# Adding the experts' rows to the residual rows in memory by accumulating transfers, instead of gathering and adding them afterwards

## The chip, the cores and the metric

The kernel runs on one core of a Trainium2 chip. The metric is the device time of one execution in microseconds, the median of three runs. TensorE is called PE here, VectorE DVE, ScalarE ACT, GpSimd POOL and SyncE SP. SBUF is the on-chip memory with 128 partitions, PSUM the memory that TensorE writes to, and HBM the large memory outside. A DMA is a transfer by the core's 16 DMA engines. It is issued by the queue of SP, ACT or POOL.

## What is computed

One transformer block with a mixture of experts is followed by a second block, whose mixer is a short convolution. All arithmetic is float32, 1024 tokens of width 1024. The part that the change touches is the routed experts, the sum of their rows into the residual stream, two norms and the first product of the second block:

```python
def expert_block(args):            # one block of 128 rows, all of one expert
    xb, e = args
    g = xb @ w_gate[e]
    u = xb @ w_up[e]
    return (jax.nn.silu(g) * u) @ w_down[e]

ys = lax.map(expert_block, (xs, block_expert)).reshape(rows, d)
out = jnp.zeros((t, d), h.dtype).at[row_token].add(ys * row_weight[:, None])
...
x = x + gate2[:, None, :] * moe
return rms_norm(x, final_norm_g)
# second block
h = modulate(rms_norm_2(x, norm_gains[i, 0]), sh_m, sc_m)
bcv = h @ w_in                     # 1024 x 3072, then the convolution
```

Each token goes to 2 of 32 experts (`TOP_K` = 2), so 2048 rows are spread over blocks of 128 rows; a block belongs to one expert and what it has over is padding. With the inputs used here 32 blocks are computed.

## The kernel before

The kernel is written by hand, engine by engine; each engine's program is a fixed list with semaphore waits, and there is no scheduler. It consists of stages, each a `nc.Block()`, which ends with a barrier of all engines: diff_attention, mla_attention, attention_out, route, experts, combine_conv, conv_out_ffn. Behind mla_attention and route stands `clear_sems` (L58), which clears the used semaphores on POOL and has a further barrier of all engines.

Products in float32 precision are made of three passes (`three_passes`, L115): each operand is split into a leading part (an ACT copy to the type fp32r) and a rest (a DVE subtraction). So every weight piece that comes from memory costs one ACT instruction and one DVE instruction before TensorE can use it.

**mla_attention.** While the attention runs, SP fills 34 blocks of the memory tensor `y_rows` with zeros (L1009, four transfers of 4352 KB).

**route (L1702).** DVE works out the experts, weights and destinations of all tokens in a chain of small instructions. Last come the list of tokens of each block (`g.rows`) and the expert of each block (`g.blocks`, from a comparison of 48 x 32 elements on one partition, L1866). SP waits for `g.blocks` and loads the first four weight pieces (L1885); POOL waits for `g.rows` and gathers the first two blocks of token rows by indirect DMAs (L1893).

**experts (L1897).** A loop on each engine, two blocks per round. One block has 12 weight pieces of 512 KB (8 of gate and up, 4 of down). SP loads a piece into one of 12 slots of `e_raw` as soon as DVE has used the slot's last content (`low`). ACT and DVE split it into one of 6 slots of `e_w` (L2122, L2058), TensorE multiplies (72 products of 128x512 for a block, besides 12 transposes). DVE's `copy_y` (L2080) takes the block's result out of PSUM, multiplied by the gate row, into `e_yo`. ACT's `store_y` (L2142) waits for that copy and issues a plain transfer of the 128 rows to `y_rows`. POOL only gathers the token rows of a block two ahead (L1990, L1993).

**combine_conv (L2188).** POOL gathers for each of 8 tiles of 128 tokens the two rows of each token from `y_rows` (16 indirect DMAs, L2263). DVE multiplies each by its weight and adds it to the residual rows (`add`, L2434 and L2437). ACT and DVE make two norms (`square_sum`, `norm`, `square_normed`, `inverse`, and ACT's `scaled`, L2353). TensorE turns the rows (`turn_half`, L2284), ACT applies scale and shift (`affine`, L2363), DVE splits (`split`, L2457 and L2459), and the first column of the input product (`f` = 0) follows. All of this goes by halves of 512 tokens: the product of a half waits until all its 8 chunks of 128 channels are split. The scale and shift come from two sums over partitions on TensorE (L69), whose operands SP loads in this stage, behind the three weight pieces of `f` = 0.

## Time and profile before

| | us |
|---|---|
| median of 3 runs | 2646.66 (2643.35 to 2647.84) |
| the profiled execution | 2647.36 |
| its span (first to last instruction) | 2645.7 |
| PE busy | 2383.6 (90%) |
| DVE busy | 1732.2 (65%) |
| ACT busy | 1229.3 (46%) |
| POOL busy | 452.0 (17%) |
| mean granted TensorE clock | 0.945 of full speed |

Times in rows count from the first instruction of the span. A row of the timeline gives the start, the duration, the engine, the line of the code, the operation, `output<-inputs`, the number of instructions, and in brackets how long the engine had been idle before and what ended that. "SPq", "ACTq" and "POOLq" are rows of an engine's queue: issues of transfers, drains and semaphore events. A share of the DMA engines is the time that packets took, added up over 16 engines, by 16 times the stretch. With all queues added it can come out a little above 100%.

### The profile page before, as it was taken

How to read it: one execution, taken by the hardware profiler on the slowest of the kernel's cores; microseconds unless marked ns; L12 is line 12 of the kernel's file. 1: busy time of each engine (PE TensorE's matmuls, PEld its weight loads, DVE VectorE, ACT ScalarE, POOL GpSimd, SP SyncE). 2: the span in 40 equal slices, each digit the busy share in tenths (PEclk: the TensorE clock that was granted, in tenths of full speed). 3: DMA queues.
4: the chain of work that ended last, by engine and by line, in shares of the span. 5: the costliest groups of instructions: out<-in, count | busy, mean ns of one | idle time of the engine just before them, and what ended most of it. 6: DMA issues, size and time to landing. Idle time of an engine off the chain costs nothing. (4 is left out here: it accounts for less than half of the span.)

```text
span 2645.7 us, 31508 instructions
## 1 busy us (share of the span) xinstructions
PE 2383.6 (90%) x10764; PEld 1908.4 (72%) x10764; DVE 1732.2 (65%) x1998; ACT 1229.3 (46%) x1643; POOL 452.0 (17%) x396
## 2 busy tenths in 40 slices
PE   5989986898897599999999569997999999999998
PEld 4667764676576488777877358886777888888886
DVE  6378884656585699999999655444447666653344
ACT  5246664565422477777676451110564333332332
POOL 0000001887200110000000200000013333221100
PEclk8999986999897799999999779998999999999999
DMA  6131121339464699999999844332423223245453
GB/s 242 28 119 49 41 87 51 97 90 340 138 204 159 243 399 398 399 398 398 399 398 399 311 153 119 112 104 79 160 76 84 79 76 91 71 139 176 149 169 116
DMA packets 266072, 485.30 MB, mean 183 GB/s; under 512 B 19633, under 2 KB 125566, under 8 KB 265470
## 3 DMA queue, kind: packets, MB, share of 16 engines
q1 hardware_dynamic: 232734, 364.37, 39.6%
q0 software_dynamic: 26912, 98.62, 11.2%
q10 hardware_dynamic: 6336, 21.11, 2.0%
q8 instruction: 57, 0.93, 0.1%
q14 instruction: 33, 0.27, 0.0%
HBM read 402.24 MB, written 76.55 MB: 181 GB/s over the span
## 5 line engine op out<-in xcount | busy, mean ns | idle before, releaser
L2058 DVE TENSOR_TENSOR e_w<-e_raw,e_w 128x1024 fp32r<-128x1024 f32 x384 | 441.9, 1219 | 55.0 <-ACT e_w L2122 54.8
L2122 ACT ACTIVATE e_w<-e_raw 128x1024 fp32r<-128x1024 f32 x384 | 376.5, 1051 | 186.0 <-PE e_pgu L119 146.2
L119 PE MATMUL e_pgu<-e_w,e_xt 128*128 128x512 f32 x1536 | 368.1, 396 | 11.1 <-DVE e_w L2058 5.5
L119 PEld LDWEIGHTS e_pgu<-e_w,e_xt 128*128 128x128 f32 x1536 | 285.3, 189 | 85.8 <-DVE e_w L2058 18.3
L119 PE MATMUL s_ps<-h,s_w 128*128 128x512 f32 x1152 | 266.8, 394 | 5.0 <-DVE h L2459 5.0
L119 PEld LDWEIGHTS s_ps<-h,s_w 128*128 128x128 f32 x1152 | 218.8, 190 | 51.8 <-DVE h L2459 5.6
L119 PE MATMUL w_ps<-w_out,w_ring 128*128 128x512 f32 x1056 | 244.1, 390 | 2.1 <-DVE w_ring L3095 2.1
L119 PE MATMUL w_ps<-y 128*128 128x512 f32 x1056 | 240.1, 389 | 1.4 <-DVE w_o_full L3260 1.0
L119 PEld LDWEIGHTS w_ps<-w_out,w_ring 128*128 128x128 f32 x1056 | 198.1, 188 | 45.1 <-DVE w_out L3102 2.9
L119 PEld LDWEIGHTS w_ps<-y 128*128 128x128 f32 x1056 | 197.9, 188 | 43.5 <-issue 1.4
L119 PE MATMUL w_ps<-y,w_ring 128*128 128x512 f32 x816 | 196.0, 398 | 4.3 <-ACT w_h L2892 3.0
L119 PE MATMUL e_py<-e_w,e_att 128*128 128x512 f32 x768 | 186.1, 398 | 3.7 <-DVE e_att L2075 3.7
L119 PEld LDWEIGHTS w_ps<-y,w_ring 128*128 128x128 f32 x816 | 154.2, 189 | 42.2 <-ACT w_h L2892 3.2
L119 PEld LDWEIGHTS e_py<-e_w,e_att 128*128 128x128 f32 x768 | 143.9, 191 | 33.5 <-issue 4.0
L119 PE MATMUL ad_pj<-h,ad_w 128*128 128x512 f32 x576 | 144.6, 406 | 4.7 <-ACT ad_spare L502 4.7
L3248 DVE TENSOR_TENSOR y<-w_o_full,y 128x1024 fp32r<-128x1024 f32 x44 | 53.9, 1225 | 143.6 <-ACT y L3032 143.6
L119 PEld LDWEIGHTS ad_pj<-h,ad_w 128*128 128x128 f32 x576 | 108.2, 192 | 38.9 <-issue 7.5
L3032 ACT ACTIVATE y<-w_o_full 128x1024 fp32r<-128x1024 f32 x44 | 46.6, 1060 | 161.4 <-PE w_ps L119 161.4
L2899 ACT ACTIVATE w_ring<-w_h 128x512 fp32r<-128x512 f32 x80 | 50.3, 632 | 143.6 <-PE w_ps L119 132.7
L3095 DVE TENSOR_TENSOR w_ring<-w_raw,w_ring 128x512 fp32r<-128x512 f32 x76 | 88.1, 1187 | 24.5 <-ACT w_ring L2899 24.5
L119 PE MATMUL w_ps<-w_out,y 128*128 128x512 f32 x384 | 94.5, 406 | 9.6 <-DVE w_out L3077 9.4
L1990 POOL COPY e_idx<-rows 128x1 uint32 x30 | 16.4, 546 | 468.0 <-PE e_px L2001 468.0
(402 smaller groups left out, 3904.4 us busy)
## 6 DMA issues: line engine op xcount, KB each, us to landing
e_raw<-in_w_expert_gate_dram SPq DMA_DIRECT2D x128, 512.0 KB, 12.7
e_raw<-in_w_expert_up_dram SPq DMA_DIRECT2D x128, 512.0 KB, 12.4
e_raw<-in_w_expert_down_dram SPq DMA_DIRECT2D x128, 512.0 KB, 12.2
w_raw<-in_ffn_w_gate_up_dram SPq DMA_DIRECT2D x48, 512.0 KB, 5.9
w_o_full<-in_ffn_w_down_dram SPq DMA_DIRECT2D x44, 512.0 KB, 4.0
y_rows<-am_zrow SPq DMA_DIRECT2D x4, 4352.0 KB, 34.7
raw_rows<-in_w_ada_dram POOLq DMA_DIRECT2D x32, 512.0 KB, 3.9
y_rows<-e_yo ACTq DMA_DIRECT2D x32, 512.0 KB, 6.3
```

The costliest lines, as they stand in the source:

```text
L119: o = pe.matmul(out, stat[i], mov[j], start=start and n == 0, stop=stop and n == 2)
L1990: pool.tensor_copy(idx[b][:], g.rows[:, ds(2 * i + b, 1)]).then_inc(idx_ready, 1)
L2058: dve.tensor_tensor(w[1][:, slot % CUT], raw[:, slot], w[0][:, slot % CUT].bitcast(F32), ALU.subtract).then_inc(low, 1)
L2122: act.activation(w[0][:, slot % CUT], raw[:, slot], ACT.Copy).then_inc(high, 1)
L2899: act.activation(ring[0][:, to], src, ACT.Copy).then_inc(high, 1)
L3032: act.activation(d_w[0][t % 2].rearrange("p (c n) -> p c n", c=2), d_raw[t % 2], ACT.Copy).then_inc(d_high, 1)
L3095: dve.tensor_tensor(ring[1][:, to], src, ring[0][:, to].bitcast(F32), ALU.subtract).then_inc(low, 1)
L3248: dve.tensor_tensor(d_w[1][t % 2].rearrange("p (c n) -> p c n", c=2), d_raw[t % 2], d_w[0][t % 2].rearrange("p (c n) -> p c n", c=2).bitca ...
```

## The change

- `y_rows`, its zero fill, the 16 gathers and the 16 DVE additions of combine_conv are gone. The memory tensors `h2_rows` and `x_rows` get 128 more rows, which take what padding rows read and write; 8 transfers clear them in mla_attention.
- route makes a further table: the weight of each slot of each block (`weight_of`, 16 products on TensorE, `g.weight_at`). The expert of each block is worked out with the blocks over the partitions (`ended`, `owner`), turned by one product (`pow_`), and stands ready before the destinations of the tokens are worked out.
- In experts `copy_y` multiplies by the slot's weight as well. ACT's `store_y` is gone. POOL scatters each block's rows by an indirect DMA with `compute_op=ALU.add` onto the residual rows in memory (`scatter`). Each scatter waits for the copy of its block and for the landing of the scatter before, since a token can be in two blocks. SP loads the residual rows when both last scatters have landed; the operands of the two sums and the gain row are loaded before that.
- combine_conv begins with the two sums. The unit rows are made by DVE (`scaled`, `tensor_scalar`) instead of ACT. TensorE turns chunk by chunk into five places of PSUM, and the product of `f` = 0 goes chunk by chunk, three columns to each, as soon as a chunk is split.
- `clear_sems` is gone; POOL clears the semaphores in the stage that follows, without a barrier of its own.

```diff
@@ mla_attention, SP
-                    sp.dma_start(g.y_dram.rearrange("(n p) (c q) -> c p n q", p=P, c=4)[q, :, MIN_BLOCKS:],
-                                 zrow[:].unsqueeze(1).broadcast_to([P, Y_BLOCKS - MIN_BLOCKS, D // 4])).then_inc(g.zeroed, 16)
+                    for rows in (g.h_dram, g.x_dram):
+                        sp.dma_start(rows[T:T + P, q * (D // 4):(q + 1) * (D // 4)], zrow[:]).then_inc(g.zeroed, 16)
@@ route, DVE
+                seq(dve.tensor_scalar(ended[:], inc[:], tok[:, NT + 1:NT + 2], None, ALU.is_le))
+                seq(dve.tensor_reduce(owner[:], ended[:], AX_X, ALU.add))
+                dve.tensor_scalar(owner[:], owner[:], float(EXPERTS - 1), None, ALU.min).then_inc(owners, 1)
...
+                dve.tensor_copy(g.blocks[0:1, 0:MAX_BLOCKS], pow_[0:1, 0:MAX_BLOCKS]).then_inc(known, 1)
...
+                dve.tensor_tensor(weight_of[:], at_block[:], bc(g.wt[:].rearrange("p s n -> p (s n)"), MAX_BLOCKS), ALU.mult).then_inc(spread, 1)
@@ experts, POOL
+                def scatter(j, b, others):
+                    pool.wait_ge(y_copied, j + 2)
+                    if not (isinstance(j, int) and j == 0):
+                        pool.wait_ge(y_out[1 - b], 16 * others)
+                        pool.sem_inc(y_free, 1)
+                    pool.tensor_copy(idy[b][:], g.rows[:, ds(j, 1)]).then_inc(idy_ready, 1)
+                    pool.wait_ge(idy_ready, j + 1)
+                    pool.sem_inc(idx_seen, 1)
+                    pool.indirect_dma_start(g.x_dram, bass.IndirectOffsetOnAxis(ap=idy[b][:], axis=0), yo[:, b, :], None,
+                                            compute_op=ALU.add).then_inc(y_out[b], 16)
...
+                with pool.Fori(0, n) as i:
+                    gather(2 * i + 6, 0)
+                    scatter(2 * i + 2, 0, i + 1)
+                    gather(2 * i + 7, 1)
+                    scatter(2 * i + 3, 1, i + 2)
@@ experts, DVE and ACT
-                    dve.tensor_tensor(yo[:, b, :], py[:], g.gate[:, 1, :], ALU.mult).then_inc(y_copied, 1)
+                    dve.wait_ge(y_free, j + 1)
+                    dve.scalar_tensor_tensor(out=yo[:, b, :], in0=py[:], scalar=g.weight_at[:, ds(j, 1)], in1=g.gate[:, 1, :],
+                                             op0=ALU.mult, op1=ALU.mult).then_inc(y_copied, 1)
...
-                def store_y(j, b):
-                    act.wait_ge(y_copied, j + 2)
-                    act.dma_start(y_rows[ds(j, 1)].squeeze(0), yo[:, b, :]).then_inc(y_out[b], 16)
@@ combine_conv, TensorE
+                for c in range(KD):
+                    turn(c)
+                pe.wait_ge(col_out, 1)
+                pe.wait_ge(low, 6)
+                for k in range(KD - 1):
+                    first_products(0, k)
+                turn(KD)
+                turn(KD + 1)
+                first_products(0, KD - 1)
...
@@ combine_conv, ACT (the order until the first affine)
+                columns()
                 square_sum(0)
                 square_sum(1)
                 square_normed(0)
                 square_sum(2)
                 square_normed(1)
-                scaled(0)
                 square_sum(3)
                 square_normed(2)
-                scaled(1)
                 leading(0, 0)
                 square_normed(3)
-                scaled(2)
                 leading(0, 1)
-                scaled(3)
-                columns()
-                affine(0)
+                square_sum(4)
                 leading(0, 2)
-                square_sum(4)
+                for c in range(4):
+                    affine(c)
```

The first place is POOL's loop in experts. `e_xg` is the buffer of token rows, `e_yo` the block's result, `x_rows` the residual rows in memory. Before, one round is:

```order
L1990 ISA
L1990 COPY e_idx<-rows 128x1
L1993 DMA e_xg<-h_rows,e_idx 128x1024
L1988 REGISTER_ALU
L1990 ISA
L1990 COPY e_idx<-rows 128x1
L1993 DMA e_xg<-h_rows,e_idx 128x1024
```

And now:

```order
L2003 COPY e_idx<-rows 128x1
L2006 DMA e_xg<-h_rows,e_idx 128x1024
L2009 REGISTER_ALU
L2011 ISA
L2013 ISA
L2013 COPY e_idy<-rows 128x1
L2014 REGISTER_ALU
L2016 DMA x_rows<-e_yo,e_idy 1152x1024
L2001 REGISTER_ALU
L2003 ISA
L2003 COPY e_idx<-rows 128x1
L2006 DMA e_xg<-h_rows,e_idx 128x1024
```

Between two gathers POOL now has the wait for a block's copy, the wait for the scatter before, and a scatter.

The second place is ACT's loop in experts, at the end of a block. `e_att` is the turned activation, `e_w` the leading parts of the weights. Before:

```order
L2138 ACTIVATE e_att<-e_pa 128x512
L2142 ISA
L2142 DMA y_rows<-e_yo 128x1024
L2121 REGISTER_ALU
L2122 ACTIVATE e_w<-e_raw 128x1024
```

And now:

```order
L2180 ACTIVATE e_att<-e_pa 128x512
L2163 REGISTER_ALU
L2164 ACTIVATE e_w<-e_raw 128x1024
L2163 REGISTER_ALU
L2164 ACTIVATE e_w<-e_raw 128x1024
```

The issue of the store, with its wait for DVE's copy, is out of ACT's queue, so that the next weight piece follows the activation directly.

The third place is TensorE at the start of combine_conv. `s_ps` and `s_pm` are PSUM, `s_mrows` and `column_parts` the operands of the two sums, `h_room` unit rows, `h_0`, `h_1` and `s_w` the split operands. Before:

```order
L69 MATMUL s_ps<-ones,s_mrows 128x1 x16
L2284 MATMUL s_pm<-ident,h_room 128x128 x32
L119 MATMUL s_ps<-h_0,s_w 128x512 x2
L119 MATMUL s_ps<-h_1,s_w 128x512
L119 MATMUL s_ps<-h_0,s_w 128x512 x2
```

And now:

```order
L60 MATMUL s_ps<-ones,column_parts 128x1 x16
L2305 MATMUL s_pm<-ident,h_room 128x128 x8
L2305 MATMUL s_ps<-ident,h_room 128x128 x12
L2305 MATMUL s_pm<-ident,h_room 128x128 x8
L2305 MATMUL s_ps<-ident,h_room 128x128 x4
L110 MATMUL s_ps<-h_0,s_w 128x512 x2
L110 MATMUL s_ps<-h_1,s_w 128x512
```

The order on TensorE up to the first product is nearly the same; the turned chunks go to more places, and the products behind it now run over the chunks first.

## Rows read from the trace of the kernel before

**Rows 1.** DMA of the stretch 890 to 1480 (experts): queues, then issues with us to landing.

```profile
DMA packets 96386, 233.92 MB, mean 396 GB/s; under 512 B 7040, under 2 KB 7040, under 8 KB 96379
...
q1 hardware_dynamic: 87739, 202.38, 90.3%
q0 software_dynamic: 4320, 15.73, 6.8%
q10 hardware_dynamic: 4320, 15.73, 6.6%
...
y_rows<-e_yo ACTq DMA_DIRECT2D x30, 512.0 KB, 6.3
...
e_xg<-h_rows,e_idx POOLq DMA_INDIRECT x30, 7.8
```

**Rows 2.** Landing times of weight pieces (tile e_raw) issued in 932 to 1000.

```profile
DMA to landing us min/median/max: 10.6/12.9/14.5
```

**Rows 3.** The same for pieces issued in 1400 to 1500.

```profile
DMA to landing us min/median/max: 9.1/11.9/14.1
```

**Rows 4.** Waits in 950 to 1450: who waited for what, us in total, times, longest.

```profile
ACT e_w L2122 <- DMA e_raw<-in_w_expert_up_dram: 0.2, 1, 0.2
```

**Rows 5.** Timeline of one block of experts, and the third last copy of a result.

```profile
1246.69 0.34 ACTq L2142 DMA_DIRECT2D y_rows<-e_yo  x1
1247.48 3.91 ACT L2122 ACTIVATE e_w<-e_raw 128x1024 fp32r<-128x1024 f32 x4 [5.25 <-PE e_pgu L119]
1248.57 9.18 DVE L2058 TENSOR_TENSOR e_w<-e_raw,e_w 128x1024 fp32r<-128x1024 f32 x8 [1.45 <-ACT e_w L2122]
...
1249.85 3.04 PE L119 MATMUL e_pgu<-e_w,e_xt 128*128 128x512 f32 x12 [0.40 <-DVE e_w L2058]
...
1255.17 1.15 POOL L1993 DMA_INDIRECT e_xg<-h_rows,e_idx  x1 [0.79 <-POOL e_idx L1990]
...
1466.78 1.22 DVE L2080 TENSOR_TENSOR e_yo<-e_py,gate 128x1024 f32<-128x1024 f32 x1
```

**Rows 6.** The copies of the results (tile e_yo): ns min/median/max, first and last start.

```profile
L2080 DVE TENSOR_TENSOR e_yo<-e_py,gate x32: 1209/1216/1225, 931.6 to 1492.4; 128x1024 f32<-128x1024 f32 x32
```

**Rows 7.** Queue rows of line 61, the barriers of clear_sems.

```profile
L61 POOLq EVENT_SEMAPHORE  x4: 17/17/17, 697.6 to 888.9; - x4
```

**Rows 8.** Queue rows of line 1750, the end of route.

```profile
L1750 POOLq EVENT_SEMAPHORE  x2: 17/17/17, 887.7 to 887.8; - x2
...
L1750 POOLq DRAIN  x1: 8389/8389/8389, 879.3 to 879.3; - x1
```

**Rows 9.** Timeline from route to experts.

```profile
872.74 1.75 DVE L1866 TENSOR_TENSOR r_cmp<-r_inc,r_marks 1x1536 f32<-1x1536 f32 x1
...
878.38 2.40 SPq L1885 DMA_DIRECT2D e_raw<-in_w_expert_gate_dram  x4
```

**Rows 10.** Landing times of the gathers (tile e_xg) issued in 870 to 900.

```profile
DMA to landing us min/median/max: 6.0/7.6/8.0
```

**Rows 11.** Timeline from experts into combine_conv.

```profile
1492.41 1.23 DVE L2080 TENSOR_TENSOR e_yo<-e_py,gate 128x1024 f32<-128x1024 f32 x1 [8.68 <-PE e_py L119]
...
1531.01 6.99 PE L69 MATMUL s_ps<-ones,s_mrows 128*128 128x1 f32 x32 [38.64 <-DMA s_mrows<-acc_sections]
...
1548.45 17.93 PE L119 MATMUL s_ps<-h,s_w 128*128 128x512 f32 x72 [2.72 <-DVE h L2459]
...
1579.93 25.28 PE L119 MATMUL s_ps<-h,s_w 128*128 128x512 f32 x99 [2.27 <-DVE h L2459]
...
1599.19 1.06 ACT L2333 ACTIVATE s_w<-s_raw 128x1024 fp32r<-128x1024 f32 x1 [4.38 <-PE s_ps L119]
```

**Rows 12.** Groups of instructions in 1496 to 1600, mean ns of one.

```profile
L2339 ACT ACTIVATE s_t<-x_rows 128x1024 f32<-128x1024 f32 x8 | 8.5, 1060 | 34.1 <-DVE x_rows L2437 34.0
L2341 ACT ACTIVATE s_ss<-s_ss,eps 128x1 f32<-128x1 f32 x8 | 2.4, 294 | 0.2
...
L2341 ACT ACT_TABLE_LOAD x1 | 1.3, 1283 | 0.0
```

More of the change, by code:

```diff
@@ L1766, in _ @@
                 o.then_inc(table, 1)
+                pe.wait_ge(spread, 3)
+                for t in range(2 * NT):
+                    o = pe.matmul(pwt[:, 0:MAX_BLOCKS], at_slot[:, t, :].bitcast(F32), weight_of[:, t, :], start=t == 0, stop=t == 2 * NT - 1)
+                o.then_inc(weighted, 1)
             @block.scalar
@@ L1778, in _ @@
                 act.wait_ge(gated, 4)
+                act.wait_ge(weighted, 1)
+                act.activation(g.weight_at[:], pwt[:, 0:MAX_BLOCKS], ACT.Copy).then_inc(done, 1)
+                act.wait_ge(done, 3)
             @block.vector
@@ L1893, in _, with experts @@
                     pool.indirect_dma_start(g.e_xg[b][:], None, g.h_dram, bass.IndirectOffsetOnAxis(ap=g.e_idx[b][:], axis=0)).then_inc(g.e_got[b], 16)
-def experts(nc, g, a, ahead):
+def experts(nc, g, a, finished, early, ahead):
     PIECES, RAW, CUT = 12, E_RAW, 6
@@ L1911, in experts @@
         raw, idx, xg = g.e_raw, g.e_idx, g.e_xg
+        idy = [sb(f"idy{b}", [P, 1], U32) for b in range(2)]
         w = [sb(f"w{j}", [P, CUT, 2, FE], F32R) for j in range(2)]
@@ L1979, in _ @@
                 load_last(2 * m + 1)
+                early(sp)
+                for b in range(2):
+                    sp.wait_ge(y_out[b], 16 * m + 16)
                 ahead(sp)
@@ new lines, in _ @@
+                gather(2, 0)
+                gather(3, 1)
+                gather(4, 0)
+                scatter(0, 0, 0)
+                gather(5, 1)
+                scatter(1, 1, 1)
+                with pool.Fori(0, n) as i:
[3 more added lines that the diff above has]
+                    scatter(2 * i + 3, 1, i + 2)
+                scatter(2 * n + 2, 0, n + 1)
+                scatter(2 * n + 3, 1, n + 2)
@@ L1995, in _ @@
+                scatter(2 * n + 4, 0, n + 2)
+                scatter(2 * n + 5, 1, n + 3)
             @block.tensor
@@ L2180, in _, with combine_conv @@
                 a_leading(j)
-                store_y(2 * m, 0)
-                store_y(2 * m + 1, 1)
-                for b in range(2):
-                    act.wait_ge(y_out[b], 16 * m + 32)
-                    act.sem_inc(all_done, 1)
-def combine_conv(nc, g, a, x_in, h_t, room, y_t, y, jobs):
+def combine_conv(nc, g, a, x_in, acc_in, sums_of, fg, h_t, room, y_t, late, jobs):
     with ExitStack() as ctx:
-        names = ("fg_in acc_in sums col_out ab x_out rows_in0 rows_in1 rows_in2 rows_in3 first added x_sq x_root x_inv normed n_sq n_root n_inv "
+        names = ("sums col_out ab x_out x_sq x_root x_inv normed n_sq n_root n_inv "
                  "unit_done turned full_done h_high h_low "
@@ L2199, in combine_conv @@
                  "part_in0 part_in1 step sec_ps sec_out")
-        (fg_in, acc_in, sums, col_out, ab, x_out, rows_in0, rows_in1, rows_in2, rows_in3, first, added, x_sq, x_root, x_inv, normed, n_sq,
+        (sums, col_out, ab, x_out, x_sq, x_root, x_inv, normed, n_sq,
          n_root, n_inv, unit_done, turned, full_done, h_high, h_low,
@@ L2258, in _ @@
             def _(pool):
-                for n in range(NT):
-                    if n >= 4:
-                        pool.wait_ge(added, n - 3)
-                    for s in range(2):
-                        pool.indirect_dma_start(y[:, n % 4, s, :], None, g.y_dram,
-                                                bass.IndirectOffsetOnAxis(ap=g.dest[:, s, n:n + 1], axis=0)).then_inc(rows_in[n % 4], 16)
                 pool.wait_ge(normed, NT)
-                pool.wait_ge(sums, 2)
                 for t in range(2):
@@ L2523, in _ @@
                 dve.tensor_copy(g.b_col[:], g.mod2[:, 0, 0:8]).then_inc(ab, 1)
-                split(0)
+                norm(0)
+                norm(1)
+                scaled(0)
+                norm(2)
+                scaled(1)
+                norm(3)
+                scaled(2)
+                rest(0, 0)
+                scaled(3)
+                rest(0, 1)
+                norm(4)
                 rest(0, 2)
-                add(4)
-                add(5)
-                norm(4)
+                for c in range(4):
+                    split(c)
                 norm(5)
-                add(6)
-                inverse(4)
-                add(7)
-                inverse(5)
+                scaled(4)
+                for c in range(4, KD):
+                    split(c)
+                scaled(5)
                 norm(6)
                 norm(7)
-                inverse(6)
-                inverse(7)
-                split(1)
+                scaled(6)
+                scaled(7)
+                for c in range(KD, 2 * KD):
+                    split(c)
                 for f in range(KD):
@@ L3396, in build @@
             with x2:
[L3397 to L3398 removed]
+                late = x2.enter_context(nc.sbuf_tensor("late_units", [P, 5, D], F32, side="right"))
                 y_at = (x_at, nc.sbuf_top)
@@ L3401, in build @@
                 with hidden:
-                    combine_conv(nc, g, a, x2_in, h_t, room, y_t, y_rows, second_sections[2:6])
+                    combine_conv(nc, g, a, x2_in, acc_in, sums_of, fg, h_t, room, y_t, late, second_sections[2:6])
                 conv_out_ffn(nc, g, a, y_t, y_at, out)
```

278 lines of the change are left out of this document (132 added, 146 removed).

## The prediction

> **What bounds the kernel now.** I began with the stage that takes the largest part of what the change touches, the experts, and asked which resource is full there. The view of DMA over this stretch answers it. The three queues together take 90.3 + 6.8 + 6.6 = 103.7% of the 16 engines' time, and 233.92 MB go at a mean of 396 GB/s [rows 1]. A block needs 12 weight pieces of 512 KB, one gather and one store of 512 KB, 7.34 MB; at 396 to 399 GB/s that is 18.4 to 18.5 us. A weight piece lands 12.9 us after its issue early in the stage and 11.9 us late in it, and never in under 9 us [rows 2, 3]. With 12 us in flight at 396 GB/s, 4.8 MB or 9 of the 12 slots are always on their way: the DMA engines never run empty.
>
> Then I looked at who waits. ACT, which takes the pieces first, waited for a transfer once, 0.2 us in 500 [rows 4]. The copy of the result recurs every (1466.78 - 931.6)/29 = 18.45 us [rows 5, 6]. Within a block TensorE has a gap of 0.4 us, ended by DVE [rows 5]; so TensorE sets the pace. Both limits lie within 1% of each other: the backlog shrank by only 12.9 - 11.9 = 1.0 us in the whole stage, so the transfers are faster than TensorE by a few hundredths of a us per block. Whatever is added to the transfers' work is therefore paid, once the slack is used up. The slack: a slot's round is 18.45 us (mean of the period), 12.4 in flight, 6.0 before and in ACT (3.91/4 = 0.98) and DVE (9.18/8 = 1.15) [rows 5]. With 2.5 for these and their handing over, some 3 us of later landing are free; with the 1.0 of backlog that now drains, 4.
>
> The second place is the way from the experts to the second block. The last copy ends at 1493.64. The first product begins at 1548.45, its first half takes 17.93 us, the second half begins at 1579.93, and `f` = 0 ends at 1599.19 [rows 11]: 105.6 us, of which 37.2 are products. The third is the way from route to experts, 12 us [rows 8, 9].
>
> **The scatter.** It takes the place of a store that costs 6.6% of 590 us by 30 = 1.30 us of all 16 engines. The gathers, which POOL issues as the scatter, cost 6.8%, or 1.34 us; so the queue alone adds 0.04 [rows 1]. No row shows an accumulating transfer. It must read the 512 KB of the destination besides the 512 KB of the source. From below this could be free, if that read runs beside other packets: 0.04 us. From above, a row is read, then added, then written, one after the other, two more passages: 2.6 us. The nearest row is that of a transfer of as many bytes, and reading is what the gather does: I take one more passage, 1.3 us. The new period is 18.45 + 1.3 = 19.75 us. Of the 32 scatters, 29 are issued before the last weight piece has landed. 29 x 1.3 = 37.7 us, less the 4 us of slack: **+34 us**.
>
> The Trainium skill has a rule for this price, on the page "Collectives: The Full Stack", section "The bandwidth ceiling: the fold count and why AG ≠ RS ≠ AR": a reducing transfer emits two read descriptors per chunk on one ring, and ran 1.93 times slower than a copy. By it, as an estimate, the extra is 0.93 x 1.30 = 1.2 us and the term +31 us. No row here shows it.
>
> **The rest of the experts' loop.** ACT loses the store, whose issue at 1246.69 (0.34 us) stood ahead of the next weight piece at 1247.48, while DVE then waited 1.45 us for ACT and TensorE 0.40 for DVE [rows 5]. So this gap of TensorE goes. What is late next is the transfers, so it brings nothing: at best 0.1 us x 30 = 3 us if the scatter is free, which I leave out. `copy_y` gets a scalar: no more than 0.1 us of DVE, which then waits 1.45 us less. POOL's scatter comes after 0.4 + 0.79 us of index copy and takes 1.15 us to issue [rows 5]. Its wait for the scatter before is over if that lands within some 16 us; a gather lands in 7.8 [rows 1]. Behind it in the queue waits a gather whose rows are needed two blocks later. This costs nothing.
>
> **mla_attention.** The zero fill is SP's alone, the loads behind it are needed only in the next stage, and nothing but POOL's side work shares the transfers with it. Taken at 0 (bounds: 0 to -2). The clearing behind this stage has a barrier of its own, as the one behind route, which lasts from 887.8 to 888.9 [rows 7, 8]. POOL now clears inside the next stage: **-1.1 us**.
>
> **Route.** The comparison on one partition (1.75 us, and a reduction as long) went at the end of DVE's chain [rows 9]; in its place come some nine small instructions before the destinations, about 2 us, and the weight table of 768 elements, half of the comparison's 1536 and so some 0.9 us, which lies beside TensorE's table. I put the list of rows at the same moment. The weight table's products end before POOL's drain, which takes 8.4 us, until the second gather has landed [rows 8, 10]. The weight pieces are now asked for 12 us earlier, so the gathers, which landed in 7.6 us beside them [rows 10], land in 6.0, the least seen: -1.6. The clearing goes: -1.1 [rows 7, 8]. **-2.7 us**; bounds 0 and -5.
>
> **From experts to `f` = 0**, counted from the last copy's end (1493.64 in before):
> - POOL: index copy and wait, 1.3 us. The last scatter issues and lands: a plain gather took at least 6.0 [rows 10], a loaded one 7.8 [rows 1]; I take 7.
> - SP issues 8 loads at 0.4 us (a plain issue took 0.34 [rows 5]), and the stage's barrier 0.5: 3.7. The next stage begins at +12.
> - The two sums now are ahead of everything on ACT: 6.99 us of cold TensorE [rows 11], +0.3: +19.3. The residual rows have landed by then.
> - ACT until the first `affine`: 5 + 4 squares and roots of 1.06 + 0.29 us and 0.2 for reading the sum, a table load of 1.3 [rows 12], three weight copies of 1.06 [rows 11]: 18.4 us. `affine` and its split 2, +1 for the last weight rest: first product at +40.7, now at +54.8.
> - 144 products: 17.9 + 19.3 us as now [rows 11], less the second of two slow starts, 1.5; 8 turnings of 0.5 us; 1.2 waiting for the last unit rows, 1.9 for the last split: 42.8.
>
> `f` = 0 ends at +83.5, now at 1599.19 - 1493.64 = +105.6: **-22 us**, bounds -15 and -28. The gap between the halves, 1566.4 to 1579.9, goes; the chain on ACT takes its place as what is late. What follows (`f` = 1) needs a weight copy and rest of 4 us after the first column, which the two other columns still cover.
>
> **The sum.** +34 - 1.1 - 2.7 - 22 = +8 us. The profiled execution took 2647.36 us, 1.7 above its span and 0.7 above the median of the runs. Against it the kernel would take 2655.6; beside the median 2654.9. I say **2655 us**.
>
> **Rivals.**
> *The read is free* (ends faster). If the engines' reads have room that writes lack, the destination's read hides behind the weights. The mechanism is in the experts' loop, its price 29 x 1.3 us, and it decides at (26 + 4)/29 = 1.0 us of extra time per block: below that the change gains. For it: the rows count bytes moved, not which side is full. Against: in 590 us with some 9 pieces waiting the queues do no more than 396 GB/s in the mean [rows 1]. Then nothing is lost, the 0.04 is in the slack, and the gains stay: 2647.4 - 26 = 2621 us (2614 to 2629). The Trainium skill, "DMA: Bandwidth & Descriptors", section Specifications, puts the ceiling at 435 GB/s; by it 7.34 + 0.52 MB take 18.1 us, under the 18.45 of TensorE, an estimate of this same case; the trace does not agree, with 396 GB/s in rows 1.
> *Part of it hides*, 0.5 to 0.9 us per block: 29 x 0.7 - 4 - 26 = -10: 2637 us.
> *It costs more than one passage*: each row's read, sum and write one after the other. At 2.6 us: 29 x 2.6 - 4 - 26 = +45: 2692 us; at 1.8 us +22: 2669 us. For it: nothing here shows how such a transfer runs. Against it: 16 engines have other packets to run meanwhile.
> *The scatters' chain stalls*: each waits for the landing before, and `copy_y` waits for that. If a scatter lands later than about 16 us beside a backlog of weights, every block is stretched by the difference. Gathers land in 7.8 beside the same backlog, so this needs twice that. At 18 us: +2 x 30 = +60 us more than the free read, 2681.
>
> **How the numbers follow.** One more passage 0.50, of it 0.34 slower, 0.12 within 0.2%, 0.04 faster (its own range 2643 to 2666, from 1.0 to 1.4 us and the bounds of the transition). Free read 0.24, faster. Partly hidden 0.12: 0.09 faster, 0.03 same. More than one passage 0.11 and stalling 0.03: slower. 0.2% are 5.3 us, about what a measurement here can tell from no change. Faster 0.37, same 0.15, slower 0.48. The range of 2617 to 2675 leaves out the costlier half of the dear cases and the edge of the free one.
>
> **What would show it.** The copies of the result in experts recur every 19.7 us instead of 18.45; ACT then waits for transfers of `e_raw`, some 0.8 to 1.3 us per block in the mean, and TensorE for DVE; weight pieces land after 15 us or more. If the period stays at 18.4 and landings stay below 14 us, the read is free and the forecast wrong. Scatters land in 7 to 11 us. From the last copy to the first product 41 us, to the end of `f` = 0 84 us. ACT sits idle in combine_conv until the sums are done. From the list of rows to the first weight copy 10 us instead of 12.6. The forecast is wrong as well if the transition gains over 28 us or under 15.

## The result and the profile after

The changed kernel takes 2631.4 us (median of 4 runs, 2627.39 to 2631.6) against 2646.7 for the kernel before: ratio 0.9941, 95% interval 0.9923 to 0.9958, so 15.3 us or 0.6% faster. I had forecast 2655 us, 8 slower. The range held the time, the direction was wrong. The profiled execution took 2631.39 us, its span is 2629.6 (before 2647.36 and 2645.7). One of the four executions of e6 (3466.9 us) and one of e7 (10898.4 us) were in a far slower state, and the medians below leave them out.

The span is 16.1 us shorter. The same marks in both profiles say where; "period" is the mean of 29 intervals between the copies of the blocks' results.

| stretch | before | after | change | forecast |
|---|---|---|---|---|
| start to the first copy of a result | 931.57 | 927.09 | -4.5 | -3.8 |
| 29 periods of the loop | 535.2 (18.46 each) | 549.2 (18.94 each) | +14.0 | +34 |
| third last copy to the last one's end | 26.9 | 25.9 | -1.0 | 0 |
| last copy's end to the end of `f` = 0 | 105.6 | 80.1 | -25.5 | -22 |
| the rest | 1046.5 | 1047.4 | +0.9 | 0 |

The other terms came out within 4 us. The loop missed by 20 us, and most of the experiments are about it.

The view of DMA over the experts stage of the changed kernel, which answers to [rows 1] (the queue q10 of the stores is gone):

```profile
DMA packets 95507, 231.14 MB, mean 385 GB/s; under 512 B 7048, under 2 KB 7048, under 8 KB 95502
...
q1 hardware_dynamic: 86862, 199.61, 84.9%
q0 software_dynamic: 8640, 31.46, 19.5%
...
e_xg<-h_rows,e_idx POOLq DMA_INDIRECT x30, 6.9
```

The scatter's packets take about twice the time of plain ones. Gather and scatter together take 19.5% of 600 us; the gather of before took 6.8% of 590. The bytes that the scatter must read at its destination are not among them (385 GB/s in 18.94 us are 7.3 MB, the 12 pieces, the gather and one passage of the scatter), so 385 GB/s is less than the engines moved: with another 0.52 MB per block it is 7.86 MB in 18.94 us, 415 GB/s. The waits over the stage (who waited for what, us in total, times, longest), where [rows 4] had 0.2 us:

```profile
ACT e_w L2164 <- DMA e_raw<-in_w_expert_gate_dram: 60.3, 87, 2.9
ACT e_w L2164 <- DMA e_raw<-in_w_expert_up_dram: 43.3, 64, 1.8
DVE e_w L2098 <- ACT e_w L2164: 39.5, 45, 2.7
```

ACT now waits for weights some 3.5 us per block. The transfers have become the limit, as forecast. Now the timeline of the same place as in [rows 5]:

```profile
1246.00 1.06 ACT L2164 ACTIVATE e_w<-e_raw 128x1024 fp32r<-128x1024 f32 x1 [1.47 <-DMA e_raw<-in_w_expert_up_dram]
...
1248.73 2.20 ACT L2164 ACTIVATE e_w<-e_raw 128x1024 fp32r<-128x1024 f32 x2
...
1249.52 1.28 DVE L2120 SCALAR_TENSOR_TENSOR e_yo<-e_py,weight_at,gate 128x1024 f32<-128x1024 f32 x1
...
1252.12 1.91 POOL L2016 DMA_INDIRECT x_rows<-e_yo,e_idy  x1 [0.81 <-POOL e_idy L2013]
```

ACT splits two weight pieces (1248.73) while DVE still copies the result (1249.52). In before ACT stood idle for 5.25 us in this place [rows 5]. The row puts the wait down to TensorE, but ACT's queue issued the store at 1246.69, and the copy for which the store waits had ended at 1246.53:

```profile
1245.32 1.21 DVE L2080 TENSOR_TENSOR e_yo<-e_py,gate 128x1024 f32<-128x1024 f32 x1
```

The copies, with the third last one, against [rows 5, 6]:

```profile
L2120 DVE SCALAR_TENSOR_TENSOR e_yo<-e_py,weight_at,gate x32: 1276/1278/1284, 927.1 to 1500.9; 128x1024 f32<-128x1024 f32 x32
```

```profile
1476.28 1.28 DVE L2120 SCALAR_TENSOR_TENSOR e_yo<-e_py,weight_at,gate 128x1024 f32<-128x1024 f32 x1
```

(1476.28 - 927.1)/29 = 18.94 us. It is not even: the first two intervals take 17.7 us, faster than any of before, the later ones 19.1 in the mean of a pair. That was the first sign that 18.45 us was no floor of before.

Route and the way into experts, which answer to [rows 8, 9]; then the landing of the first two gathers, which answers to [rows 10]:

```profile
865.25 2.09 SPq L1895 DMA_DIRECT2D e_raw<-in_w_expert_gate_dram  x4
...
876.13 0.19 DVE L1885 CAST rows<-r_free 128x48 uint32<-128x48 f32 x1
...
885.16 2.01 ACT L2164 ACTIVATE e_w<-e_raw 128x1024 fp32r<-128x1024 f32 x2 [2.44 <-DMA m_sec<-in_w_ada_dram]
```

```profile
DMA to landing us min/median/max: 4.3/4.8/5.3
```

The weights are asked for 13 us earlier and have landed before the gathers start; the gathers land in 4.3 to 5.3 us (forecast 6.0), and from the list of rows to the first weight copy it is 9.0 us (forecast 10, before 12.6). The transition, which answers to [rows 11]:

```profile
1500.88 1.28 DVE L2120 SCALAR_TENSOR_TENSOR e_yo<-e_py,weight_at,gate 128x1024 f32<-128x1024 f32 x1 [7.61 <-PE e_py L110]
...
1503.44 1.57 POOL L2016 DMA_INDIRECT x_rows<-e_yo,e_idy  x1 [0.78 <-POOL e_idy L2013]
...
1509.64 4.01 SPq L3420 DMA_DIRECT2D x_rows<-x_rows  x8
...
1514.25 6.96 PE L60 MATMUL s_ps<-ones,column_parts 128*128 128x1 f32 x32 [13.51 <-PEq L1950]
...
1542.25 14.54 PE L110 MATMUL s_ps<-h,s_w 128*128 128x512 f32 x63
...
1573.65 52.00 PE L110 MATMUL s_ps<-h,s_w 128*128 128x512 f32 x228 [2.06 <-DVE h L2482]
...
1582.22 1.06 ACT L2376 ACTIVATE s_w<-s_raw 128x1024 fp32r<-128x1024 f32 x1 [1.66 <-PE s_ps L110]
```

From the last copy's end (1502.16): sums at +12.1 (forecast +12), first product at +40.1 (+40.7), end of `f` = 0 at +80.1 (+83.5).

### The profile page after: what moved, and what is told of

Its sections match the earlier page's. It is cut to its first block and busy times, and to the rows that moved or that the text cites. A ratio compares the mean times of both kernels' runs of the same rounds, so it can differ in the third digit from the quotient of the medians.

```text
span 2629.6 us, 31677 instructions
## 1 busy us (share of the span) xinstructions
PE 2377.8 (90%) x10798; PEld 1911.2 (73%) x10798; DVE 1727.5 (66%) x1993; ACT 1248.6 (47%) x1636; POOL 512.0 (19%) x444
## 5 line engine op out<-in xcount | busy, mean ns | idle before, releaser
L2098 DVE TENSOR_TENSOR e_w<-e_raw,e_w 128x1024 fp32r<-128x1024 f32 x384 | 451.2, 1221 | 55.9 <-ACT e_w L2164 50.6
L2164 ACT ACTIVATE e_w<-e_raw 128x1024 fp32r<-128x1024 f32 x384 | 405.4, 1060 | 144.2 <-DMA e_raw<-in_w_expert_gate_dram 60.3
L110 PEld LDWEIGHTS w_ps<-w_out,y 128*128 128x128 f32 x384 | 73.0, 192 | 30.0 <-DVE w_out L3096 11.8
```

The costliest lines, as they stand in the source:

```text
L110: o = pe.matmul(out, stat[i], mov[j], start=start and n == 0, stop=stop and n == 2)
L2098: dve.tensor_tensor(w[1][:, slot % CUT], raw[:, slot], w[0][:, slot % CUT].bitcast(F32), ALU.subtract).then_inc(low, 1)
L2164: act.activation(w[0][:, slot % CUT], raw[:, slot], ACT.Copy).then_inc(high, 1)
```

## The experiments

All runs are of whole kernels; where one leaves out or changes a part of the result, its expectation says so. "Period" is the mean of 29 intervals between copies, as above, "GB/s" the mean over 1000 to 1400, "landing" the median time in us from issue to landing of a weight piece issued there. The ratio is to executions of before that were taken beside each run, whose median lay between 2646.6 and 2648.5 us.

| run | us | ratio to before (95%) | period | GB/s | landing |
|---|---|---|---|---|---|
| before | 2646.7 | | 18.46 | 399 | 12.4 |
| after | 2631.4 | 0.9941 (0.9923 to 0.9958) | 18.94 | 384 | 12.0 |
| e1_plain_scatter | 2590.6 | 0.9784 (0.9768 to 0.9800) | 17.69 | 413 | 11.9 |
| e2_add_hold | 2630.9 | 0.9937 (0.9921 to 0.9954) | 18.95 | 384 | 12.4 |
| e3_plain_hold | 2602.4 | 0.9828 (0.9812 to 0.9844) | 18.01 | 410 | 7.3 |
| e4_no_scatter | 2586.8 | 0.9766 (0.9750 to 0.9783) | 17.68 | 385 | 5.4 |
| e5_act_store | 2616.2 | 0.9880 (0.9863 to 0.9896) | 18.51 | 397 | 6.0 |
| e6_act_store_late | 2588.9 | 0.9780 (0.9760 to 0.9799) | 17.69 | 413 | 12.2 |
| e7_extra_gather | 2628.6 | 0.9935 (0.9915 to 0.9955) | 18.94 | 413 | 13.5 |
| e8_half | 2640.4 | 0.9979 (0.9970 to 0.9989) | 18.94 | 384 | 12.6 |
| e9_before_late_store | 2639.8 | 0.9966 (0.9953 to 0.9978) | 18.31 | 399 | 13.8 |
| e10_skip_gather | 2631.3 | 0.9935 (0.9920 to 0.9950) | 18.86 | 372 | 12.3 |
| e11_same_padding_row | 2590.8 | 0.9783 (0.9768 to 0.9798) | 17.68 | 413 | 12.6 |
| e12_two_rows | 2629.7 | 0.9927 (0.9914 to 0.9941) | 18.28 | 400 | 13.3 |
| e13_after_shifted | 2647.5 | 1.0003 (0.9993 to 1.0012) | 19.46 | 375 | 13.1 |
| e14_before_late_shifted | 2621.6 | 0.9906 (0.9891 to 0.9921) | 17.70 | 413 | 12.7 |
| e15_before_late_memory | 2641.7 | 0.9978 (0.9969 to 0.9988) | 18.34 | 399 | 13.9 |
| e16_two_rows_b | 2603.1 | 0.9838 (0.9824 to 0.9851) | 17.69 | 413 | 11.9 |
| e17_others_shifted | 2632.6 | 0.9943 (0.9926 to 0.9961) | 18.94 | 384 | 11.7 |
| e18_after_shifted_64 | 2646.7 | 0.9998 (0.9989 to 1.0008) | 19.46 | 375 | 13.0 |

**Addition and hold, two by two.** Two accounts stood against each other. Theory A: before was limited by the transfers, and the addition costs only half a passage. Theory B: before was held up by ACT's wait for the copy and its store, and the addition costs a whole passage. The first four runs take the accumulation and ACT's wait apart. The plain scatter (e1) and ACT's wait (e2; e3 has both edits):

```diff
-  ... yo[:, b, :], None, compute_op=ALU.add).then_inc(y_out[b], 16)
+  ... yo[:, b, :], None).then_inc(y_out[b], 16)
@@ ACT, end of step(j)
                     a_leading(j)
+                    act.wait_ge(y_copied, j + 1)
```

> The changed kernel, with the scatter as a plain write: it does not add to the rows in memory but overwrites them (the result lacks the sum). Everything else stays, so ACT has no store and no wait for the copy. Theory A (the transfers were full at 18.45 us per block; the destination's read costs 0.65 us of the 1.3, the rest of it hides): without the read the period of the copies returns to 18.4 to 18.5 us, and the time is 29 x 0.5 = 14 us under the changed kernel, about 2617 us. Theory B (before was held at 18.45 by ACT's wait for the copy and its store, the transfers had about 0.7 us per block to spare, and the read costs the whole 1.3 us of a passage): the period is 17.7 us, as in the first three blocks of the changed kernel, and the time about 2631 - 29 x 1.24 = 2595 us.

> The changed kernel, accumulating as it does, but ACT waits at the end of each block's list for DVE's copy of the block's result, as it did for its store. Theory A: the transfers are the limit at 19.1 us per block; the first three blocks take 18.45 instead of 17.7, and the rest stays: +2 us or less, 2631 to 2634 us. Theory B: the same where the transfers have a backlog to hide the hold; if hold and transfers add up because ACT takes pieces later, up to 19.8 us per block and 2650 us.

> Plain scatter (overwrites, result lacks the sum) and ACT's wait for the copy: the experts' loop of the kernel before, but for the engine that issues the store. Both theories: a period of 18.4 to 18.5 us and about 2617 us. Only the pair with the plain scatter without the wait tells them apart: Theory A says no difference between the two, theory B 0.75 us per block or 22 us.

In e4 the scatter's transfer is replaced:

```diff
-                    pool.indirect_dma_start(g.x_dram, ..., compute_op=ALU.add).then_inc(y_out[b], 16)
+                    pool.sem_inc(y_out[b], 16)
```

> The changed kernel without the scatters' transfers (the experts' rows reach memory nowhere; the semaphore is raised by POOL itself). Theory A: the transfers lose a passage of 1.3 us from 18.45 and the engines' own limit of 17.7 shows, 2595 us. Theory B: the same 17.7 us, 2595 us, no different from the plain scatter. If the period falls under 17.6, the engines' own limit is lower than the first three blocks show.

Theory B held in e1; e2 and e4 fit both. Without the addition every block takes 17.69 us, not 18.4, and 41 us go. ACT's wait costs 0.31 us per block beside plain transfers (e3) and nothing beside accumulating ones (e2), where the transfers are the limit. Both theories missed e3: they had 18.4 to 18.5 us and 2617 us for it, and it took 18.01 and 2602.4. The wait alone does not make the pace of before; what is missing is the store (e5, below). Leaving the scatter out altogether gains nothing more in the loop (the 4 us between e4 and e1 lie outside it): 17.69 us is the engines' own pace. What ACT waits for in e1, in 950 to 1400:

```profile
ACT e_w L2163 <- PE e_pgu L110: 50.3, 177, 0.4
```

No wait for a transfer, and always 0.3 us for TensorE. This is what a loop bound by TensorE looks like; before had a wait of 5.3 us per block in this place. The share of the DMA queues, which I had read as "full", does not show that. In e4 the queues of the stretch 1000 to 1400 and the landing of its weight pieces are

```profile
q1 hardware_dynamic: 62219, 142.47, 94.9%
q0 software_dynamic: 3168, 11.54, 7.1%
```

```profile
DMA to landing us min/median/max: 3.8/5.4/7.3
```

102% again, though the queues have time to spare: the period is that of e1 with 0.52 MB less to move.

**ACT's store.** e5 has the changed kernel with the store of before, e6 the same store behind the next two weight pieces:

```diff
@@ ACT, end of step(j), e5
                     a_leading(j)
+                    store_y(j - 1, b)      # wait for the copy, plain transfer to y_rows
@@ e6
                     a_leading(j)
+                    leading_gu(j + 1, (6, 7))
+                    store_y(j - 1, b)
```

> The changed kernel with the loop's store of the kernel before: ACT waits for the copy and issues a plain transfer of the block's 128 rows to a tensor of their own; POOL keeps the waits and index copies of the scatter but issues none (the rows are not added to the residual, the result lacks them). The runs so far gave 17.69 us per block without a wait on ACT and 18.01 with the wait alone. If ACT's list is what set the pace of before, the issue itself adds the rest: 18.45 us per block and 2590.6 + 29 x 0.76 = 2613 us. If the accumulating queue or the scatter matters otherwise and the issue costs nothing, 18.0 us and 2602.

> As the run with ACT's store, but the store stands two weight pieces later in ACT's list, where the copy of the block is done or nearly done (plain rows to a tensor of their own, not added to the residual). If ACT's place for the store was the cost: 17.7 us per block, 2591 us, with the same transfers. If the store's issue or its transfer on ACT's queue costs by itself wherever it stands: 18.1 to 18.45 us, 2602 to 2613.

Both as expected: 18.51 us with the store in its old place, 17.69 two pieces later. So in the changed kernel, without the addition, the place of one instruction in ACT's list is worth 0.8 us per block; I had valued it at 0.1 at most. In e5 the pieces land in 6.0 us at the pace at which they land in 12.4 in before. A landing time of 12 us does not show that the transfers set the pace: in e1 it is 11.9 us and nobody waits for them. But what made the difference between e5 and before? The same late store in the kernel before:

> The kernel before, with one edit: ACT's store of a block stands two weight pieces later in its list. If only ACT's place for the store set the pace (ceiling of the transfers 413 GB/s, as the plain scatter showed): 17.7 us per block and 2646.7 - 29 x 0.76 = 2625 us. If the transfers of before have a lower ceiling than those of the changed kernel (its weight pieces land in 12.4 us, those of the changed kernel with the same store in 6.0): 18.4 us and 2645 us, and something else in it, such as the padding rows that all read the same row, takes transfer time.

It gained 7 to 9 us, not 22: 18.31 us per block. The transfers of before do have a lower ceiling. The waits for weights show it (950 to 1400, one of three such rows):

```profile
ACT e_w L2122 <- DMA e_raw<-in_w_expert_up_dram: 38.9, 78, 1.8
```

Of its intervals the first four are short (17.7 to 17.9 us). The copies after the fourth and after the 28th interval start at

```profile
1004.09 1.21 DVE L2080 TENSOR_TENSOR e_yo<-e_py,gate 128x1024 f32<-128x1024 f32 x1
...
1446.82 1.22 DVE L2080 TENSOR_TENSOR e_yo<-e_py,gate 128x1024 f32<-128x1024 f32 x1
```

and (1446.82 - 1004.09)/24 = 18.45 us, the period of before. So before had two limits at the same place: ACT's wait and store (18.51 us, e5) and its transfers (18.45 us, e9).

**The price of an accumulation.** e7 puts a plain read of 512 KB in the place of the destination's read; e10 takes the gathers' padding rows away.

```diff
@@ e7, POOL's gather(j, b); scatter plain as in e1
+                    pool.wait_ge(more, 16 * j - 32)
+                    pool.indirect_dma_start(spare[:], None, g.h_dram, ... idx[b] ...).then_inc(more, 16)
@@ e10, all gathers
-  ... g.h_dram, bass.IndirectOffsetOnAxis(ap=idx[b][:], axis=0))
+  ... g.h_dram[0:T, :], bass.IndirectOffsetOnAxis(ap=idx[b][:], axis=0), bounds_check=T - 1, oob_is_err=False)
```

> Plain scatter (overwrites, the sum is missing) and one more gather of 512 KB per block into a buffer that nobody reads. It puts a read of 512 KB in the place of the read that an accumulation needs. If an accumulating transfer costs what a passage of 512 KB more costs, the period is that of the changed kernel, 18.9 to 19.1 us, and the time 2590.6 + 29 x 1.3 = 2628 us, with about 412 GB/s moved. If a read runs beside the rest and accumulation is dear for another reason (its packets' own time), the period stays under 18.2 us and the time under 2606.

> The changed kernel, but the gathers skip the padding rows (half of all rows; the buffers are cleared once before); the scatter still adds all 128 rows. By the ceiling of 413 GB/s the transfers of a block are 6.29 MB of weights, 0.26 of gather and 1.05 of the scatter with its read: 7.6 MB, 18.4 us per block, 2631.4 - 29 x 0.54 = 2616 us. If the bytes are not what counts, but the number of descriptors or the weights' queue alone: no change, 2631 us.

e7 has the period of the changed kernel to 0.01 us. In e7 no transfer adds, so the view of 1000 to 1400 counts all bytes:

```profile
DMA packets 66930, 165.35 MB, mean 413 GB/s; under 512 B 5056, under 2 KB 5056, under 8 KB 66930
```

An accumulating transfer costs here what a passage of 512 KB more costs, 18.94 - 17.69 = 1.25 us; with the buffer's address of before (below) it is 19.46 - 18.31 = 1.15 (e13, e9). The forecast's 1.3 was near. The skipped rows brought 0.08 us per block instead of 0.54 and no time, 2631.3 us against 2631.4: the second account came true, by which the bytes are not what counts. With 0.52 MB for the destination's read, e10 moves (372 GB/s x 18.86 us = 7.02) + 0.52 = 7.54 MB per block, 400 GB/s, and not 413. So a ceiling in GB/s does not hold for every mix of transfers. Why fewer bytes did not help stays open; no run tests, for one, whether the skipped rows, the last of each block, relieve only some of the 16 engines.

**Why the ceiling rose.** Where the transfers are at their limit or close to it, the changed kernel and its variants reach 412 to 415 GB/s, before, e9 and e12 (below) 399 to 400. (e3, e4 and e5 move 410, 385 and 397 because their engines ask for no more; e10 is the exception above.) One row for all padding is not it: e11 is e6 with the padding rows gathering one and the same row, as in before, and keeps its 17.7 us.

```diff
@@ e11, route: padding reads row T
-  ... prt[:], 0.0, tok[:, NT:NT + 1], ALU.is_equal, ALU.mult
+  ... prt[:], 0.0, float(T + 1), ALU.is_equal, ALU.mult
@@ e15, kernel before with the late store
+  h2_rows and x_rows declared with T + P rows
@@ e13 (32 words), e18 (16 words) in after, e14 (32 words) in before with the late store
+            expert_in.enter_context(nc.sbuf_tensor("e_pad", [P, 32], F32))
             g.e_raw = expert_in.enter_context(...)
@@ e17, after: the same 32 words behind e_raw
```

> The run with ACT's late store (2589 us, 17.69 us per block), but all padding rows gather one and the same row of memory, as in the kernel before. If that is why the transfers of before are slower: over 18 us per block, 2600 us or more. If not: 17.7 us and 2589 us.

> The changed kernel with 128 unused bytes per partition ahead of the weight buffer e_raw, so that it starts 128 bytes off a multiple of 256 as in the kernel before (27904 becomes 28032). Theory of the address: the ceiling falls from 412 to about 399 GB/s, the period from 19.1 to 7.86 MB by 399 = 19.7 us, as the forecast had it, and the time to 2631.4 + 29 x 0.6 = 2649 us. Theory of the place in memory, or anything else: no change, 2631 us.

> The kernel before with the late store on ACT (18.44 us per block at 399 GB/s, 2639.8 us) and 128 unused bytes ahead of e_raw, so that it starts at a multiple of 256 as in the changed kernel. Theory of the address: the ceiling rises to 413 GB/s, the period falls to 17.7 us and the time to 2639.8 - 29 x 0.62 = 2622 us. Otherwise 18.4 us and 2640.

> The kernel before with the late store on ACT, and the tensors h2_rows and x_rows 128 rows longer (unused), so that all that follows them lies 1 MB further on in memory, as in the changed kernel; SBUF as it was. Theory of the address in SBUF: no change, 18.44 us and 2640 us. Theory of the place in memory: 17.7 us and 2622 us.

> The changed kernel with 128 unused bytes behind the weight buffer, so that e_raw stays at a multiple of 256 bytes and the buffers behind it (token rows, split weights, result) are where they were in the shifted run of 2647.5 us. If it is e_raw's own address that counts: 18.94 us per block in the mean, 2631 us. If it is that of the other buffers: 19.46 us and 2647 us.

> The changed kernel with 64 unused bytes ahead of e_raw (27968, 64 bytes past a multiple of 256). If any address off a multiple of 256 has the lower ceiling: 19.46 us per block, 2647 us. If only whether the address is a multiple of 64 counts, no change against the changed kernel: 2631 us (but the shift by 128 has already spoken against that). If the loss grows with the splitting of smaller units, more than 2647 us.

It is the address of the weight buffer. The small tables that stay in SBUF grew by 128 bytes with the change (`weight_at` came, the destinations went), and with them the start of `e_raw` moved from 27776 to 27904 bytes in each partition, from 128 bytes off a multiple of 256 to a multiple. Shifted back (e13) the changed kernel loses all its gain; shifted forward (e14) the kernel before with the late store gains 18 us. Shifting the memory tensors (e15 beside e9) or the buffers behind `e_raw` (e17) changes next to nothing (2 and 1 us), and 64 bytes off is as bad as 128 (e18). The first queue of the view of 1000 to 1400, changed kernel:

```profile
q1 hardware_dynamic: 57635, 131.74, 84.1%
```

and shifted (e13):

```profile
q1 hardware_dynamic: 56218, 129.09, 84.9%
```

That is 0.841 x 400 / 131.74 = 2.55 us of all engines per MB of weights against 2.63, 3% more. Only runs whose transfers are at or close to their limit can be compared so: in e4, at the good address but with time to spare, the same sum gives 0.949 x 400 / 142.47 = 2.66. The same view of before with the late store (e9), then shifted (e14):

```profile
DMA packets 65826, 159.46 MB, mean 399 GB/s; under 512 B 4869, under 2 KB 4869, under 8 KB 65826
```

```profile
DMA packets 68320, 165.16 MB, mean 413 GB/s; under 512 B 5049, under 2 KB 5049, under 8 KB 68320
```

The Trainium skill has a rule for this, on the page "DMA: Bandwidth & Descriptors", section "How a descriptor splits into AXI transactions": a descriptor is cut at multiples of 256 bytes, and when it does not start at one, its first transaction starts at the multiple below, and the bytes ahead of the start are fetched unused. The page tells it of reads; here the buffer is what the transfer writes to. The direction agrees with these runs. By that rule, as an estimate, 2048 bytes would be 9 transactions for 8; the 3% here are less than an eighth. No run shows single transactions, so that the cutting is the mechanism is not shown; that the address is the cause is.

**Chunk by chunk.** e8 holds the first half's products until its 8 chunks are split.

```diff
@@ first_products(h, k)
-                    pe.wait_ge(h_low, KD * h + k + 1)
+                    pe.wait_ge(h_low, KD * h + (k + 1 if h else KD))
```

> The changed kernel, but the products of the first half of f = 0 wait until all 8 chunks of the half are split, as in before; in the second half they go chunk by chunk. In the changed kernel the first product starts at 1542.25 and the eighth split of the half ends at 1550.8. If the chunk order is what brought TensorE forward there, this kernel is 8.5 us slower, 2640 us. If what is late behind it (the unit rows of the second half, split by 1573) hides that, less than 3 us slower.

9.0 us slower, as the first account said. TensorE's gap before the first product in e8, which the changed kernel does not have:

```profile
1547.07 16.26 PE L110 MATMUL s_ps<-h,s_w 128*128 128x512 f32 x63 [8.49 <-DVE h L2482]
```

So of the transition's 25.5 us some 9 come from the order of the first half's products.

**A version without accumulation.** Each token gets two rows in memory, one per expert; a second list (`rows_out`) gives the place, the scatter is plain, and combine_conv loads and adds.

```diff
@@ route: which slots are second choices
+  for n in range(NT): pe.matmul(pwt[:, MAX_BLOCKS:2 * MAX_BLOCKS], at_slot[:, NT + n, :], token_at[:, NT + n, :], ...)
+  rows_out = rows + (T + P) * (that table > 0)
@@ experts, POOL
-  pool.indirect_dma_start(g.x_dram, ..., compute_op=ALU.add)
+  pool.indirect_dma_start(g.y_dram, ...)                 # idy from rows_out
@@ combine_conv, DVE (e12: the first addition on POOL for n > 0)
+  dve.tensor_tensor(row(n, 0), row(n, 0), row(n, 1), ALU.add)
+  dve.tensor_tensor(g.x[:, n, :], g.x[:, n, :], row(n, 0), ALU.add)
```

> A version with plain scatters that computes the whole result: a token's first and second expert row go to two rows of their own (a second list in route tells which), the residual rows are loaded while experts ends, and combine_conv loads the 16 tiles of expert rows; POOL adds each pair and DVE adds the pair to the residual. Experts as with the plain scatter: 17.7 us per block, which gave 2590.6 us. In combine_conv the tiles arrive 2.6 us apart from about +16 us behind the last copy, DVE takes 3.5 us per tile and ACT 2.7: first product at +38 to +44 us behind the last copy (40 in the changed kernel), and the second half's additions take DVE 5 us, of which part may show. 2588 to 2602 us, and I say 2594. If the pairs on POOL hold the second half up, 2605.

> The version with two rows per token and plain scatters (2629.7 us: 18.28 us per block at 400 GB/s, and DVE's instructions in combine_conv took 3.2 us instead of 1.3 while POOL added beside them), now with e_raw at a multiple of 256 and both additions on DVE. Theory of the address: 17.7 us per block. From the last copy to the first product: loads land about 18 us behind it, 4 tiles of 4.8 us on DVE and 3.7 us of weight rests, 44 to 46 us; the second half's additions cost 5 to 8 us more. 2590.6 + 5 + 7 = 2603 us. If the address is not what counts: 2620 us.

e12 missed by 36 us. Two things were found: the longer list of tables had moved `e_raw` off again (by 192 bytes; period 18.28, 17 us over 29 blocks), and POOL's additions slowed DVE. POOL's additions and one multiplication by the gain in e12, then the same multiplication in e16:

```profile
1505.90 6.54 POOL L2312 TENSOR_TENSOR h_pairs<-h_pairs 128x1024 f32<-128x1024 f32 x2 [0.21 <-DMA h_pairs<-y_rows]
...
1507.06 3.18 DVE L2502 SCALAR_TENSOR_TENSOR x_rows<-x_rows,s_ss,final_gain 128x1024 f32<-128x1024 f32 x1
```

```profile
1487.80 1.28 DVE L2496 SCALAR_TENSOR_TENSOR x_rows<-x_rows,s_ss,final_gain 128x1024 f32<-128x1024 f32 x1
```

e16 has both mended and takes 2603.1 us, the 2603 expected; no run has one of the two alone. It computes the whole result and is 28 us faster than the changed kernel and 44 faster than before, the fastest of the complete kernels here. Its first product comes 48.4 us after the last copy's end (expected 44 to 46), in a profiled execution of 2611.3 us, the slowest of its five.

## Why the forecast was wrong

- **The failed step** is the term for the scatter: "The new period is 18.45 + 1.3 = 19.75 us ... +34 us". It came out as 18.94 us and +14. The 1.3 us were near (1.25 in e7, 1.15 at the old address). The base was wrong: 18.45 us was carried over to the changed kernel, and there it is 17.69 (e1).
- The base has two parts. "TensorE sets the pace" was a misreading: ACT's wait for the copy and its store made 18.45 (e5: 18.51, e6: 17.69). The row was in the forecast, an idle 5.25 us of ACT per block [rows 5], and I dismissed it as worth "at best 0.1 us". The engines' own pace is 17.69.
- That alone would not have moved the forecast, for the transfers were the other half of it, and "within 1%" was right: those of before allow 18.45 us (e9). But the change moves the buffer's address, and the ceiling rises from 399 to about 413 GB/s. No step of the forecast looked at addresses.
- With the address as it was (e13) the period is 19.46 and the stretch of 29 periods costs (19.46 - 18.46) x 29 = 29 us, near the forecast's 34; the kernel takes 2647.5 us, no change against before. The address gives 0.52 x 29 = 15 us back, which is the whole gain. That the change came out faster is luck: it lies in the size of two small tables.
- **What would show it** was half right: ACT does wait for weights, 3.5 us per block and not 0.8 to 1.3, and copies come every 18.94 us, not 19.7. Pieces do not land after 15 us but after 12.
- **Rest of the loop**: "costs nothing" held for POOL and DVE. ACT's freed place was worth nothing beside the accumulation, as e2 shows, but the 17.7 us of the first two intervals are its doing.
- **mla_attention, clearing, route**: -4.5 us for -3.8. The gathers landed faster than I took; the weights had landed before them.
- **Experts to `f` = 0**: -25.5 us for -22, each mark within 3.4 us. The chain on ACT behind the sums is late next, as said.
- **The rivals**: the time fell between "the read is free" (2621) and "partly hidden" (2637), 6 us from the latter, but the whole passage is paid (e1, e7). The number is near, the mechanism is another.

## What to carry to other kernels

An idle gap of one engine that recurs in every round is the first thing to price in a loop, even if another engine looks busy all the time: move the waiting instruction two places and see. A busy share near 100% does not show that transfers are full (e4), and a long landing time does not show that they set the pace (e1); a run with less or more to transfer does. And before blaming or crediting a change of a DMA-bound loop, compare the start addresses of the large buffers in both kernels: here a shift of 128 bytes was worth the whole gain.

## What was new about the hardware

- Where transfers are the limit, weight pieces whose buffer starts 128 or 192 bytes off a multiple of 256 in SBUF move at 399 to 400 GB/s together with the rest (e9, e12), at a multiple at 413 (e7, e14). With accumulating scatters, whose reads are not counted, it is 375 GB/s at 64 or 128 bytes off (e18, e13) against 384 (e17).
- An accumulating scatter of 512 KB costs as much transfer time as a plain scatter and a gather together (e7); the bytes read at the destination are not counted in the view. POOL takes 1.9 us to issue one in the loop, 1.3 for a plain scatter (e1) and 1.15 for a gather (before).
- DVE's multiplication of 128x1024 took 3.18 us instead of 1.28 beside an addition on POOL. The Trainium skill, "SBUF — State Buffer", section "Who interferes with whom", names a port pair of SBUF that DVE and GpSimd share; by it a DVE instruction with two inputs in SBUF and a GpSimd instruction that reads SBUF do not run together, and the second one waits for the end of the first. These rows agree: DVE's instruction is 1.9 us longer while POOL's runs.
